# A mixed attention and state-space model on one core: input tables of the recurrence layer made in the projection in front, recurrence on pairs of blocks, and each feed-forward layer's modulation vectors summed within it

## The chip, the cores and the metric

The kernel runs on one core of a Trainium2 chip. The metric is the device time of one execution in microseconds (us), taken as the median of several runs. The core has four compute engines with a queue each: TensorE (PE, matrix products; PEld is its weight load), VectorE (DVE), ScalarE (ACT) and GpSimd (POOL). SyncE (SP) issues transfers. Engines run in parallel and order themselves by semaphores.

## The reference, cut to what matters

Ten layers work on 512 tokens of width 1024 in float32: feed-forward (f), latent attention with a short convolution (m), a mixer with two attentions (e) and one with a retention and a linear state-space recurrence (o). Their order is f0 m1 f2 f3 m4 f5 e6 f7 o8 f9. Every layer normalises, scales by (1 + scale) and shifts; its result is added with a gate. Shift, scale and gate (each 1024 long) are products of an activated vector `c` with a matrix, so 28 vectors of 1024 x 1024 matrix work beside the layers.

```python
for l in range(DEPTH):
    mod = jnp.split(c_act @ w_ada[l] + b_ada[l], N_MOD, axis=-1)
    h = modulate(rms_norm(x, ffn1_norm[l]), mod[0], mod[1])
    x = x + 0.5 * (1 + mod[2])[:, None, :] * swiglu(h, ffn1_w_gu[l], ffn1_w_down[l])
    ...
# the state-space part of the recurrence layer: 32 groups of 16 channels, 64 complex states each
a_bar = jnp.exp(lam * step)
b_bar = ((a_bar - 1.0) / lam)[..., None] * b
bu = jnp.einsum('gnp,blgp->blgn', b_bar, u)
states: s[t] = a_bar * s[t-1] + bu[t]
y = jnp.einsum('gpn,blgn->blgp', c, states).real + d_skip * u
```

Beside it in the same layer: retention over four heads (scores times a decay table, times values), a gate, a gated linear unit on y, and the output projection.

## The kernel before, in words

All weights stream through two slots `raw` of 128 x 1024 (a unit, 512 KB). Float32 products are made as three products of rounded parts: ScalarE rounds a unit to `w_hi` (`split_hi`), VectorE subtracts to `w_lo` (`split_lo`), TensorE multiplies (`mm3`: 24 matmuls of 128x512 a unit, about 5.45 us at the full clock). A unit's w_hi may be written once the unit two before is used, so each of the three engines has about one unit of time for its part, and an engine that is late with unit n stops TensorE at unit n.

A feed-forward layer has a hidden loop (`pe_ffn`, `dve_ffn`, 22 hidden tiles, two units each) and an output projection (`pe_out`, `act_out`, `dve_out`: 8 tiles of three units, after each tile x gets its addition, the next layer's rounded input and the sum of squares are begun). The next layer takes this input before the norm is known (`pair_pe`) and the rest behind it.

The modulation vectors are summed on GpSimd (`mod_sums`, lines 636 to 680): for each of a layer's jobs (vector j of set s) eight tiles of 128x1024 are loaded through two slots `mod_w`, multiplied by a column (L671, the first one L667 into the accumulator) and added to `mod_acc` (L674, L677), which has three slots, by j. A tile is fetched one ahead within a vector, and the first of the next only when the last vector is summed. GpSimd starts when the layer's last low part of the normalised input is made. VectorE folds each finished vector in the hidden loop, behind fixed hidden tiles (`FOLD_AT`: 6, 9, 12, 15, 18, 21; L593 transposes, L594 sums 32 columns); TensorE spreads the folded ones (`mod_spread`) and VectorE turns them to coefficients (`mod_coef`) behind the hidden loop. Before, layer 0 has seven jobs, layers 2, 5 and 7 six, layer 3 three, layer 9 none; the last job of the long lists is folded in the output projection.

In the recurrence layer (`pe_odd`, `act_odd`, `dve_odd`, and `pool_odd` for its transfers) 16 projection units of the input stream run with the state-space work between them. 512 tokens are 64 blocks of eight (`HOP`). Tables: `s_pw` powers of a_bar, `s_g` their products with the input factor (both made in the output projection of f7 by `state_powers`), `s_m` (input weights: `weights`, L2057 twice and L2495, plus a copy of the last power to `s_fb`), turned by TensorE (L2210) and read to `s_w`; `s_ca` (output weights, `readout`, 12 operations). `inputs` (L2226) multiplies the tables with the layer's input, which went through DRAM for a new layout (L2149, L2154), to one state input per block. `scan` (L2520 to L2528) carries the 128 x 32 states over the blocks: two products, two sums per step, each waiting for the one before. `taps` (L2239) makes the within-block kernel, that also goes through DRAM (L2163, L2167); `outputs` (L2259, L2263) needs it and the states. `scores`, `decay` (L2551), `retain` are the retention; `rotate` makes its rotary products from `swap_halves`. All orders on the four queues are written out by hand; `dve_odd` has the scan in pieces between the splits of later units.

## Time and profile before

| | us |
|---|---|
| median of 3 runs | 3488.41 |
| lowest and highest | 3487.97, 3494.15 |
| the profiled execution | 3492.11 |
| its span in the trace | 3489.3 |
| busy: TensorE, VectorE, ScalarE, GpSimd | 3284.6, 1866.2, 1181.4, 984.8 |

In the trace hidden loops of f0, f2, f5 and f7 run from about 66, 720, 1734 and 2438 us, the output projection of f7 from about 2680, the recurrence layer from 2805 to 3061, f9 from there to the end. Times in brackets in a row are the idle time of the engine just before it and who ended it. A matmul's own duration is longer than its share, since matmuls overlap.

### The profile page before, as it was taken

To read this page: it belongs to the slowest core of one execution; us is meant where nothing else is said; L and a number is where in the kernel's file an instruction comes from. 1 tells how busy PE (TensorE), PEld (TensorE's weight loads), DVE (VectorE), ACT (ScalarE), POOL (GpSimd) and SP (SyncE) were. 2 spreads that over 40 slices of the span, in tenths; PEclk is the share of its full clock that TensorE was granted. 3 is DMA by queue.
4 is the path that set the end of the run, shared out by engine and by line. 5 is a ranking of instruction groups with operands and counts; after the bars stand their busy time and mean duration, and the time that the engine had idled before them with its cause. 6 is when DMAs were issued, how large, how long until landed. Compare 5 with 4: busy or idle time off the path is not lost.

```text
span 3489.3 us, 40287 instructions
## 1 busy us (share of the span) xinstructions
PE 3284.6 (94%) x14477; PEld 2616.8 (75%) x14477; DVE 1866.2 (53%) x2573; ACT 1181.4 (34%) x1778; POOL 984.8 (28%) x675
## 2 busy tenths in 40 slices
PE   6999999999999999999999998989999988899998
PEld 4887875678787888775788776757777876778887
DVE  5565455656445533555655443256677486264443
ACT  3222243532223222335422223354333231243332
POOL 2888000068803700000088600000886000000000
PEclk7999999999999999999999998989999997799999
DMA  6665342156634633331266533202665333123332
GB/s 207 204 196 178 94 133 62 37 173 198 193 97 140 192 96 93 83 87 31 85 198 199 158 95 103 79 1 72 188 199 164 94 115 67 50 84 95 97 91 90
DMA packets 576560, 420.29 MB, mean 120 GB/s; under 512 B 28716, under 2 KB 535963, under 8 KB 575303
## 3 DMA queue, kind: packets, MB, share of 16 engines
q1 hardware_dynamic: 537330, 286.09, 27.9%
q0 software_dynamic: 33952, 122.70, 11.9%
q10 hardware_dynamic: 5172, 10.17, 0.9%
q8 instruction: 58, 0.95, 0.1%
q14 instruction: 48, 0.39, 0.0%
HBM read 413.10 MB, written 8.68 MB: 121 GB/s over the span
## 4 chain that ended last, share of the span: by engine, by line
PE 62%; POOL 15%; DVE 12%; issue 4%; ACT 3%; DMA 3%; ACTq 0%; SPq 0%; DVEq 0%; POOLq 0%
PE bank L324 18%; PE bank L326 17%; PE bank L325 17%; POOL mod_acc L674 8%; POOL mod_w L671 4%; PE bank L1306 2%; POOL mod_w L643 2%; DVE tmp L449 2%; DMA mod_w<-in_w_ada 2%; PE bank L1337 2%; DVE w_lo L305 1%; DVE h_lo L459 1%; POOL mod_acc L677 1%; PE bank L1327 1%; PE bank L430 1%
## 5 line engine op out<-in xcount | busy, mean ns | idle before, releaser
L324 PE MATMUL bank<-h_hi,w_hi 128*128 128x512 f32 x2656 | 1054.1, 397 | 62.3 <-DVE w_lo L305 25.5
L325 PE MATMUL bank<-h_lo,w_hi 128*128 128x512 f32 x2656 | 1043.4, 393 | 0.0
L326 PE MATMUL bank<-h_hi,w_lo 128*128 128x512 f32 x2656 | 1042.9, 393 | 0.0
L305 DVE TENSOR_TENSOR w_lo<-raw,w_hi 128x1024 fp32r<-128x1024 f32 x438 | 650.6, 1486 | 539.1 <-ACT w_hi L288 536.9
L288 ACT ACTIVATE w_hi<-raw 128x1024 fp32r<-128x1024 f32 x438 | 462.1, 1055 | 657.0 <-PE bank L326 654.6
L324 PEld LDWEIGHTS bank<-h_hi,w_hi 128*128 128x128 f32 x2656 | 503.0, 189 | 196.5 <-issue 45.7
L326 PEld LDWEIGHTS bank<-h_hi,w_lo 128*128 128x128 f32 x2656 | 502.8, 189 | 107.9
L325 PEld LDWEIGHTS bank<-h_lo,w_hi 128*128 128x128 f32 x2656 | 503.1, 189 | 102.5
L674 POOL TENSOR_TENSOR mod_acc<-mod_acc,mod_w 128x1024 f32<-128x1024 f32 x168 | 456.3, 2716 | 14.0
L324 PE MATMUL bank<-hid_hi,w_hi 128*128 128x512 f32 x1056 | 413.9, 392 | 7.1 <-DVE w_lo L305 7.1
L326 PE MATMUL bank<-hid_hi,w_lo 128*128 128x512 f32 x1056 | 412.1, 390 | 0.0
L325 PE MATMUL bank<-hid_lo,w_hi 128*128 128x512 f32 x1056 | 412.1, 390 | 0.0
L643 POOL DMA_DIRECT2D mod_w<-in_mod_w x96 | 56.6, 589 | 1000.0 <-DVE h_lo L459 975.7
L671 POOL TENSOR_SCALAR mod_w<-mod_w,cact 128x1024 f32<-128x1024 f32 x196 | 264.2, 1348 | 13.0 <-DMA mod_w<-in_w_ada 2.2
L296 DVE TENSOR_TENSOR w_lo<-raw,w_hi 128x1024 fp32r<-128x1024 f32 x92 | 112.5, 1224 | 265.9 <-ACT w_hi L279 265.4
L643 POOL DMA_DIRECT2D mod_w<-in_w_ada x128 | 75.3, 588 | 595.7 <-DVE h_lo L459 560.7
L324 PEld LDWEIGHTS bank<-hid_hi,w_hi 128*128 128x128 f32 x1056 | 198.9, 188 | 50.1 <-DVE w_lo L305 8.7
L326 PEld LDWEIGHTS bank<-hid_hi,w_lo 128*128 128x128 f32 x1056 | 198.9, 188 | 41.8
L325 PEld LDWEIGHTS bank<-hid_lo,w_hi 128*128 128x128 f32 x1056 | 199.0, 188 | 41.0
L1171 DVE TENSOR_TENSOR hid_lo<-hid,hid_hi 128x512 fp32r<-128x512 f32 (+1 forms) x127 | 169.3, 1333 | 36.6 <-ACT hid_hi L1090 36.6
L1166 DVE TENSOR_TENSOR hid<-act_t,bank 128x512 f32<-128x512 f32 x127 | 86.8, 683 | 151.5 <-PE bank L326 151.5
L1086 ACT ACTIVATE act_t<-bank 128x512 f32<-128x512 f32 x85 | 50.8, 598 | 321.4 <-PE bank L326 321.3
(339 smaller groups left out, 3262.4 us busy)
## 6 DMA issues: line engine op xcount, KB each, us to landing
raw<-in_ffn_w_gu SPq DMA_DIRECT2D x176, 512.0 KB, 4.0
mod_w<-in_w_ada POOLq DMA_DIRECT2D x128, 512.0 KB, 4.0
mod_w<-in_mod_w POOLq DMA_DIRECT2D x96, 512.0 KB, 4.2
raw<-in_ffn_w_in SPq DMA_DIRECT2D x88, 512.0 KB, 3.7
raw<-in_ffn_w_down SPq DMA_DIRECT2D x64, 512.0 KB, 3.5
raw<-in_w_in SPq DMA_DIRECT2D x34, 512.0 KB, 3.7
raw<-in_ffn_w_out SPq DMA_DIRECT2D x32, 512.0 KB, 3.5
raw<-in_ffn_w_down SPq DMA_DIRECT2D x32, 384.0 KB, 3.1
```

Source lines behind the costliest of these rows:

```text
L288: loop(nc.scalar.activation(w_hi[:, u % 2, :], raw[:, u % 2, :], ACT.Copy), "split_hi", times)
L296: done(nc.vector.tensor_tensor(w_lo[:, u % 2, :], raw[:, u % 2, :], w_hi[:, u % 2, :].bitcast(F32), ALU.subtract), "split_lo")
L305: loop(nc.vector.tensor_tensor(w_lo[:, u % 2, :], raw[:, u % 2, :], w_hi[:, u % 2, :].bitcast(F32), ALU.subtract), "split_lo", times)
L324: nc.tensor.matmul(dst, a_hi, b_hi, start=start, stop=False)
L325: nc.tensor.matmul(dst, a_hi, b_lo, start=False, stop=False)
L326: return nc.tensor.matmul(dst, a_lo, b_hi, start=False, stop=stop)
L449: done(nc.vector.scalar_tensor_tensor(tmp[:, m % 3, :], src(m), gain(m), inv, ALU.mult, ALU.mult), "norm_scaled", (key, m))
L643: pool.dma_start(mod_w[:, slot, :], src).then_inc(sg.sem(f"mod_loaded{slot}"), 16)
L671: done(pool.tensor_scalar(w, w, c, 1.0, ALU.mult, ALU.mult), "mod_step")
L674: done(pool.tensor_tensor(acc, acc, w, ALU.add), "mod_step")
L1166: loop(nc.vector.tensor_tensor(hid[:, jj, :], act_t[:, jj, :], psum[up][:, :], ALU.mult), "pair_evac", times)
L1171: loop(nc.vector.tensor_tensor(tile(hid_lo, i * 2 + jj), hid[:, jj, :], tile(hid_hi, i * 2 + jj).bitcast(F32), ALU.subtract), "hid_lo", times)
```

## The change

Modulation: every feed-forward layer now makes its own gate, and shift and scale (and for a mixer the gate too) of the sets that follow. Layers 0, 2, 5 and 7 have six jobs, layer 3 three, layer 9 one; all are folded in the hidden loop. The accumulator has two slots in turn, the tile buffer three, and tiles are fetched two ahead, across vectors. Recurrence layer: the four input tables are made in the output projection of f7, behind the splits 1, 2, 4, 5 of its second pair of tiles, into four slots of their own; the copies to s_fb are dropped (taps reads the tables); `combine` first makes each block's input that of two blocks, then the scan goes on pairs of blocks with the squared factor, in 31 steps; the orders on TensorE, ScalarE and VectorE are written anew.

```diff
-        mod_acc = place("mod_acc", [P, 3 * D])
-        mod_w = place("mod_w", [P, 2, D])
+        mod_acc = place("mod_acc", [P, 2 * D])
+        mod_w = place("mod_w", [P, 3, D])
...
         def mod_jobs(key):
-            if key[0] != "f" or key == final:
+            if key[0] != "f":
                 return []
             n = ORDER.index(key[1])
-            if n == 0:
-                return [(0, 2)] + [(t, j) for t in (ORDER[1], ORDER[2]) for j in range(3)]
-            ahead = {("f", 2): (1, 2), ("f", 3): (2,), ("f", 5): (1, 2), ("f", 7): (1, 2)}[key]
-            return [(ORDER[n + k], j) for k in ahead for j in range(3)]
+            jobs = [(ORDER[n], 2)]
+            for t in (n + 1, n + 2):
+                kind = [k for k, s in PHASES if k != "b" and t < len(ORDER) and s == ORDER[t]]
+                if kind == ["f"]:
+                    jobs += [(ORDER[t], 0), (ORDER[t], 1)]
+                elif kind and not (t == n + 1 and n and ("f", ORDER[n - 1]) in PHASES):
+                    jobs += [(ORDER[t], j) for j in range(3)]
+            return jobs
...
+        def mod_sums(pool, key):
+            for n, (s, j) in enumerate(jobs):
+                if n == 0:
+                    wait(pool, "norm_lo", (key, KT - 1))
+                    fetch(0, 0)
+                    fetch(0, 1)
+                if len(turn.former) >= 2:
+                    wait(pool, "mod_folded", turn.former[-2])
+                turn.former.append((s, j))
+                for t in range(KT):
+                    if t + 2 < KT:
+                        fetch(n, t + 2)
+                    elif n + 1 < len(jobs):
+                        fetch(n + 1, t + 2 - KT)
...
             def body(i, times):
-                if isinstance(i, int) and i == 2 and len(jobs) > 3:
-                    mod_fold(dve, key, len(jobs) - 1)
-                if isinstance(i, int) and i == 3 and len(jobs) > 3:
-                    mod_coef(dve, jobs[-1][0], [0, 1, 2], 7)
+                if isinstance(i, int) and i == 3 and len(sets) > 2:
+                    mod_coef(dve, sets[2], set_parts(key, sets[2]), 7)
...
+                        if ahead and isinstance(i, int) and i == 1 and k in (1, 2, 4, 5):
+                            state_weights(dve, nxt, (1, 2, 4, 5).index(k))
...
-            folding = FOLD_AT[:len(jobs) - (len(jobs) > 3)]
+            folding = FOLD_AT[:len(mod_jobs(key))]
...
+                cmul((den, t), power(HOP), power(HOP), s_t[:, :, 0])
+        def state_weights(dve, nxt, x):
+            part, js = x // 2, slice(8 * (x % 2), 8 * (x % 2) + 8)
+            if x == 0:
+                wait(dve, "b_loaded", nxt)
+            m = [s_m[:, i, :].rearrange("p (j k c) -> p j k c", j=8, k=HOP) for i in (x, 4)]
+            for i in range(2):
+                tt(m[i], spread(s_g[:, (i + part) % 2, js, :], 3, 16), spread(s_b[:, i, js, :], 2, HOP))
+            done(nc.vector.tensor_tensor(m[0], m[0], m[1], ...), "weights_ready", (nxt, x))
...   (pe_odd)
             readout()
-            weights(0)
+            for x in range(4):
+                weights(x)
             unit(4)
-            weights(1)
             unit(5)
+            inputs()
+            wait(pe, "out_ready", key)
             swap_halves(0)
-            weights(2)
+            swap_halves(1)
             unit(6)
-            wait(pe, "out_ready", key)
-            swap_halves(1)
-            weights(3)
-            inputs()
+            swap_halves(2)
             unit(7)
-            swap_halves(2)
             swap_halves(3)
+            wait(pe, "rotated", (key, 1))
             unit(8)
...   (dve_odd)
+            def combine():
+                n = BLOCKS - 2
+                former, now = s_s[:, :, :, 1:BLOCKS - 1], s_s[:, :, :, 2:BLOCKS]
+                vstep(nc.vector.tensor_tensor(s_q[:, 0, :, :, :], former, spread(s_a[:, 0, 0, :, :], 3, n), ALU.mult))
+                vstep(nc.vector.tensor_tensor(s_q[:, 1, :, :, :], swapped(former, n), spread(s_a[:, 0, 1, :, :], 3, n),
+                                              ALU.mult))
+                vstep(nc.vector.tensor_tensor(now, now, s_q[:, 0, :, :, :], ALU.add))
+                vstep(nc.vector.tensor_tensor(now, now, s_q[:, 1, :, :, :], ALU.add))
...
-            weights(0)
             split_lo(dve)
-            weights(1)
-            split_lo(dve)
-            weights(2)
-            split_lo(dve)
-            rotate(0)
-            weights(3)
-            split_lo(dve)
-            rotate(1)
             readout(0)
             split_lo(dve)
             readout(1)
+            split_lo(dve)
+            split_lo(dve)
             wait(dve, "input_read", (key, 3))
-            scan(2, 6)
+            combine()
+            split_lo(dve)
+            rotate(0)
+            rotate(1)
             split_lo(dve)
             rotate(2)
-            scan(6, 8)
             rotate(3)
-            scan(8, 11)
+            scan(0, 3)
             split_lo(dve)
-            scan(11, 16)
+            scan(3, 7)
             split_lo(dve)
-            scan(16, 21)
+            scan(7, 12)
             split_lo(dve)
-            scan(21, 37)
+            scan(12, 20)
             split_lo(dve)
-            scan(37, 42)
+            scan(20, 25)
             split_lo(dve)
-            scan(42, 47)
-            split_lo(dve)
+            scan(25, STEPS)
             wait(dve, "decay_loaded", key)
             wait(dve, "taps_stored", key)
             decay(0)
-            scan(47, 50)
             decay(1)
-            scan(50, BLOCKS)
+            split_lo(dve)
             gate_head(0)
```

ScalarE reads the eight table banks in one piece behind unit 3 and the state inputs behind unit 5. `scan(first, last)` now counts steps, each over blocks i and i + 1 with i = 3 + 2 * step.

## Rows read from the trace of the kernel before

**Rows 1.** The page: busy time, share of the span and instructions of each engine.
```profile
PE 3284.6 (94%) x14477; PEld 2616.8 (75%) x14477; DVE 1866.2 (53%) x2573; ACT 1181.4 (34%) x1778; POOL 984.8 (28%) x675
```
**Rows 2.** Who waited for whom, whole span: total us, times, longest.
```profile
DVE tmp L593 <- POOL mod_acc L677: 17.7, 3, 7.1
```
**Rows 3.** Timeline of TensorE, recurrence layer: start, us, instructions, [idle before, releaser].
```profile
2876.38 0.80 PE L356 MATMUL bank<-w_hi,h_hi 128*128 128x512 f32 x1 [5.02 <-DVE w_lo L296]
...
2918.20 2.42 PE L2273 MATMUL bank<-o_qk 64*128 64x512 f32 x8
2926.74 4.63 PE L2273 MATMUL bank<-o_qk 64*128 64x512 f32 x8 [6.11 <-DVE o_w L2551]
...
2943.49 3.65 PE L2259 MATMUL bank<-s_u,s_taps 128*128 128x64 f32 x16 [5.25 <-DVE s_s L2528]
...
2964.26 4.77 PE L2263 MATMUL bank<-s_s,s_ca 64*128 64x64 f32 x32
...
2983.19 7.09 PE L2263 MATMUL bank<-s_s,s_ca 64*128 64x64 f32 x32
```
**Rows 4.** Windows: stretch, us, busy time of each engine, granted clock, DMA.
```profile
2860.00:2880.00 20.00, 14.98 (x55) 11.05 (x54) 19.24 (x39) 2.60 (x3) 0.00 (x0) 0.87 0.17 53
...
2920.00:2940.00 20.00, 12.13 (x28) 6.97 (x27) 12.65 (x60) 2.25 (x3) 0.00 (x0) 0.66 0.28 75
```
**Rows 5.** Timeline of VectorE, projection of f7 and recurrence layer.
```profile
2703.38 0.23 DVE L2057 TENSOR_TENSOR s_pw<-s_pw 128x64 f32<-128x64 f32 x1
...
2847.33 2.48 DVE L2057 TENSOR_TENSOR s_m<-s_g,s_b 128x1024 f32<-128x1024 f32 x2
...
2872.16 0.20 DVE L2520 TENSOR_TENSOR s_p<-s_s,s_a 128x32 f32<-128x32 f32 x1
...
2872.89 0.20 DVE L2520 TENSOR_TENSOR s_p<-s_s,s_a 128x32 f32<-128x32 f32 x1
```
**Rows 6.** Timeline of GpSimd, then the issues of all transfers (KB, median us to landing).
```profile
2837.81 5.00 POOL L2154 DMA_DIRECT2D s_u<-bias_skewed_rows  x8 [5.95 <-DMA bias_skewed_rows<-o_u]
...
s_u<-bias_skewed_rows POOLq DMA_DIRECT2D x8, 128.0 KB, 4.2
```
**Rows 7.** Who waited for whom: GpSimd's first product of a vector.
```profile
POOL mod_acc L667 <- DMA mod_w<-in_w_ada: 45.4, 16, 3.2
```
**Rows 8.** Timelines in layer 2: VectorE, GpSimd's last addition, TensorE behind the fifth fold.
```profile
923.70 1.25 DVE L593 STREAM_TRANSPOSE tmp<-mod_acc 128x1024 f32<-128x1024 f32 x1 [7.12 <-POOL mod_acc L677]
...
951.78 0.69 DVE L1171 TENSOR_TENSOR hid_lo<-hid,hid_hi 128x512 fp32r<-128x512 f32 x1
...
962.56 3.25 POOL L677 TENSOR_TENSOR mod_acc<-mod_acc,mod_w 128x1024 f32<-128x1024 f32 x1
...
927.47 0.49 PE L324 MATMUL bank<-h_hi,w_hi 128*128 128x512 f32 x1 [2.97 <-DVE w_lo L305]
```
**Rows 9.** Layer 0, behind the hidden loop: timeline of TensorE and one window.
```profile
315.72 0.79 PE L324 MATMUL bank<-hid_hi,w_hi 128*128 128x512 f32 x1 [4.46 <-DVE w_lo L305]
...
346.07 0.51 PE L324 MATMUL bank<-hid_hi,w_hi 128*128 128x512 f32 x1 [2.37 <-DVE w_lo L305]
...
300.00:320.00 20.00, 15.47 (x62) 12.35 (x59) 12.22 (x16) 4.98 (x6) 16.00 (x11) 0.87 0.53 163
```
**Rows 10.** Layers 7 and 9: VectorE at their starts, TensorE behind a fold.
```profile
2435.90 1.62 DVE L459 SCALAR_TENSOR_TENSOR h_lo<-tmp,coef,h_hi 128x512 fp32r<-128x512 f32 x2
...
2446.01 3.36 DVE L305 TENSOR_TENSOR w_lo<-raw,w_hi 128x1024 fp32r<-128x1024 f32 x1
...
2458.87 1.64 DVE L305 TENSOR_TENSOR w_lo<-raw,w_hi 128x1024 fp32r<-128x1024 f32 x1 [0.96 <-ACT w_hi L288]
...
2588.41 0.49 PE L324 MATMUL bank<-h_hi,w_hi 128*128 128x512 f32 x1 [1.97 <-DVE w_lo L305]
...
3123.17 1.62 DVE L459 SCALAR_TENSOR_TENSOR h_lo<-tmp,coef,h_hi 128x512 fp32r<-128x512 f32 x2
...
3140.39 1.23 DVE L305 TENSOR_TENSOR w_lo<-raw,w_hi 128x1024 fp32r<-128x1024 f32 x1 [2.28 <-ACT w_hi L288]
```

More of the change, by code:

```diff
@@ L2530, in scan @@
-                    if i < BLOCKS - 1:
+                    ins = nc.vector.tensor_tensor(now, now, p2, ALU.add)
+                    final_step = step == STEPS - 1
+                    done(ins, "scanned" if final_step else "scan_step", key if final_step else None)
+                    if not final_step:
                         dve.wait_ge(sg.sem("scan_step"), sg.count["scan_step"])
```

172 lines of the change are left out of this document (75 added, 97 removed).

## The prediction

> **What bounds the kernel now.** I read the page first. TensorE is busy for 94% of the span and no other engine reaches 60% [rows 1], so only three things can shorten the time: fewer idle gaps of TensorE, more of it at the higher clock, or fewer matrix columns. The change leaves the columns alone. TensorE has 205 us without work. Second view, who waited for whom: most of TensorE's waits are for VectorE, above all for w_lo, the low parts of the weights, and VectorE in turn stood 17.7 us, three times, before a fold of a modulation vector that GpSimd had not finished [rows 2]. Third, TensorE's timeline, read only for rows with a bracket: the recurrence layer (about 2805 to 3061) has the largest cluster, 5.02 us before a w_lo, 6.11 us before a decay product, 5.25 us before the end of the recurrence [rows 3]. The clock says more than the gaps: the granted clock was 0.87 of 2.4 GHz between 2860 and 2880 and 0.66 between 2920 and 2940, that is for two thirds of that stretch at the lower level of 1.2 GHz [rows 4]. The same eight score matmuls took 2.42 us without and 4.63 us behind the 6.11 us gap [rows 3].
>
> **Part 1, the recurrence layer.** VectorE's queue is the cause of these gaps. Before, it holds four input tables of three 1024-element operations each (1.24 us apiece) with a short copy, 4 x 3.9 = 15.7 us; then 62 steps of four dependent 32-element operations, one step every 0.73 to 0.75 us, 46 us [rows 5]. After, the tables are gone from here; the steps are 31 on 64 elements; four products and sums over 1984 elements come first. A 64-element operation took 0.23 us against 0.20 for 32 [rows 5], so I take 0.85 us a step: 26 us. The four large ones by the rate of the 1024-element row, 2.2 us each: 9 us. VectorE loses 15.7 + 46 - 35 = 27 us. (The Trainium skill, Vector Engine (DVE) Microarchitecture Reference, section 5.2, has pairs of words that start on an odd word at 1.30 ns a column and a hop at every element at up to 1.98. The pairs here start at odd blocks. By that a step on pairs costs only 4 x 20 ns over one on single blocks, 0.83 us, and a large operation 2.7 us rather than 2.2; the sum would move by 1 us. No row here shows odd pairs.)
>
> What TensorE gets of it, walked unit by unit with the rows' durations. Up to the third projection unit behind the values: the 5.02 us wait, one of 1.06 behind it and the slow restart (0.13 of 20 us [rows 4] and, by my estimate, 0.8 behind it, 3.4 us) go, 9.5 us in all. New small waits come in their place: all eight table transposes now stand in one piece and are read by ScalarE one by one (1 us); unit 5's w_lo is queued behind the first readout (0.7 us); the half swap directly behind unit 6 waits for ScalarE's evacuation (0.8 us); unit 8 may not start until the second rotation, behind which VectorE now has the four large operations (0.5 us). Net -6.5 us. Then the scores: the decay product is no longer queued behind a w_lo that waits for a late load, so the gap of 6.11 becomes the 1.7 us that the product itself takes, -4.3; the second scores at full speed, -2.2; the recurrence ends some 10 us before it is needed, so the 5.25 us wait goes. Sum -18.3. The retention matmuls behind (about 7 us) have run at the lower clock; no row decides whether gaps of 1.7 us let it fall, so I count most of half their time, -3. The output products of the state stay at the lower level: a block of them took 7.09 us with full-speed work and no gap two blocks in front of it [rows 3]. Part 1: -21, with ends at -8 (every saved gap is half refilled) and -35 (the higher clock holds through the output products too).
>
> Of the steps that move: the matmuls that apply the tables now come one unit earlier, at about 2848. Their input is loaded by GpSimd's eight transfers, issued 2837.8 to 2842.8 with a median of 4.2 us to landing [rows 6]; they land at about 2848. This is hidden by nothing any more: it costs 0 to 1 us, and each us that they are late stalls TensorE and, through the wait for the products, VectorE with all splits behind it.
>
> **Part 2, the tables in the projection in front.** Twelve operations of 1.24 us stand between the splits of the second pair of output tiles (near 2710). A table is 3.7 us. One unit of TensorE is 5.45 us, ScalarE and VectorE need 2.5 of it, so 2.9 are free: a table overruns this by 0.8, and where the tile's addition comes next (2.9 us) its split comes 1 us late. Twice: +2 us (0 to 6). Ten more operations of 0.2 us for the squared factor are hidden. The two loads of b are landed some 9 us before their first use.
>
> **Part 3, the modulation vectors.** GpSimd waits for the first tile of each vector, 45.4 us in 16 times for one of the two sources [rows 7], 2.9 us each. Fetching two ahead removes it for all but the first vector of a layer: five times 3.0, so the sixth ends 15 us earlier. In layer 2 the fifth fold waited 7.12 us, TensorE 2.97 behind it [rows 8]. GpSimd then ends the fifth 12 us earlier: the wait is gone. But the sixth fold moves from the output projection into the hidden loop at tile 21. Without the 2.97 VectorE is there at 952.4 - 3.0 = 949.4 [rows 8]; GpSimd, that ended at 965.8, ends at 950.8. VectorE waits 1.5 us, folds 2.5, makes four coefficient parts in 1.7 and splits; TensorE needs that split at about 957.3 and gets it then. I allow 0.6 us. Layers 2 and 5: -2.3 each, -4.6.
> Layer 0: the first gap (4.46 us) stands behind the last fold, for which VectorE waited 17.7 - 2 x 7.12 = 3.5 us [rows 2, 9]; it shrinks to 0.6. The stretch at 0.87 [rows 9] gives 2.6 back and what lies behind it, again by estimate, 0.8. The 2.37 us gap [rows 9] falls into the seventh vector's time, when GpSimd slows w_lo; the seventh vector has left this layer. -3.9 - 3.4 - 2.4 = -9.7.
> Layer 7 (with the convolution) folds five vectors in its hidden loop and stalls each time, 1.97 us in the row shown [rows 10]; a sixth is added: +1.7.
> Layer 9 gets a vector of its own, so GpSimd works in its first 40 us, which it did not. The twin is layer 7: there w_lo took 3.36 us beside GpSimd's additions, and the split that follows the first converted pair came at 2458.87, 21.4 us after the end of the last h_lo; in layer 9 at 3140.39, 15.6 us after [rows 10]. That is +5.8 if all of it is GpSimd; layer 9 entered at the lower clock, so I take +5, and +1.6 for its fold. +6.6. (The Trainium skill, SBUF - State Buffer, section "SBUF: two separate sides", has this as an exclusive lock between GpSimd and a VectorE operation with two SBUF inputs, held for the whole instruction. It speaks against putting any of GpSimd's work beside a start that is tight. By that rule a w_lo could wait for a whole addition at each step; the trace has it at 3.36 against 1.24 us.)
> Part 3: -4.6 - 9.7 + 1.7 + 6.6 = -6.0.
>
> **Sum.** -21 + 2 - 6.0 = -25 us on the profiled execution's 3492.1 (span 3489.3 and 2.8 around it): 3467.1. The median of the runs is 3.7 below this execution, so 3463.4.
>
> **The rivals.** (a) The clock stays up: the recurrence layer no longer stands idle for more than 3 us before the output products, and these and the two projection units between them run at 2.4 GHz. For it: the second block of output products took 4.77 us right after a full-speed unit [rows 3]. Against it: the later ones took 7.09 with no gap in front [rows 3]. Price: three blocks at 3.5 to 4 us, two units at 2.5: -10 to -17 more, 3446 to 3453. (b) New waits take the place of the old: input_loaded lands 2 to 5 us late, the values' read, the gate of the second rotation, and each gap over 2.5 us pays 1.4 to 3.4 us of slow clock. Part 1 shrinks to -8, the total to -8 to -14: 3474 to 3480. (c) The state path from taps to projection outputs (two round trips through DRAM) sets the layer's end whatever VectorE does; part 1 is near 0, and layer 7 and 9's losses eat the rest: within 7 us, about 3485. Against it: TensorE waited for VectorE and not for a load in the rows of group 3. (d) Slower: GpSimd does not get faster, because its two loads in flight share the DMA engines with the weights and land later, or because its operations are held up by VectorE as long as they save. Then the sixth fold at tile 21 in layers 2 and 5 finds its vector 965.8 - 949.4 = 16.4 us late, all inside a loop in which TensorE has 4 us of cover (7.12 us of waiting cost 2.97): 12.4 + 3.4 of slow clock, twice, +32; against -25 + 4.6 for the rest this ends at +11, 3500. It decides as soon as a vector takes over 38.8 us on average (40.9 now, 38.4 by my sum); at 39.5 it costs 8 us. (e) The change does not do what it says: the tables or coefficients are made later than used and a semaphore wait shows it; the order of the queues leaves no such wait that I can find, and it would look like (c).
>
> **Chances.** Forecast 0.55; (a) 0.17; (b) 0.14; (c) with (e) 0.08; (d) 0.06. A measurement of this kernel can tell about 0.2%, 7 us, from no change. Faster: forecast, (a), (b) = 0.86; within: 0.08; slower: 0.06. The forecast's own bounds are 3453 to 3475; the range takes in all of (a) but its best end and (b): 3446 to 3480, which leaves out (c), (d) and a sliver, under 2 in 10.
>
> **What would show it.** In the recurrence layer: no TensorE gap over 2.5 us before the output products except the one at the values' read, which the change does not touch; first output products near 2925 + the shift from before; scanned no releaser of TensorE. Vectors of GpSimd 37 to 38 us apart, with no wait at their first product but in the first of a layer; VectorE's wait before folds at most 2 us. In layer 9 a gap of some 4 us at its start. Wrong if: the step on pairs takes over 1.1 us; if the eight input loads release TensorE; if the clock before 3000 is near 1.0, which is (a); if w_lo waits in layer 7's output projection exceed 3 us each.

## The result and the profile after

The kernel after takes 3458.61 us (median of four runs, 3449.83 to 3465.99) beside 3491.28 of before, a ratio of 0.9905 (95% interval 0.9878 to 0.9932). Run again on another chip it was 3454.08 beside 3496.27, 0.9880 (0.9864 to 0.9897). The forecast was 3463.4 with a range of 3446 to 3480 and 0.86 on faster: both hold. As a change the forecast was -25 us, and the medians moved by -32.7 and -42.2, each beside before on its own chip: a ratio of 0.9928 was forecast, which lies within the first interval and outside the second. The profiled execution is the fastest of its four runs (3449.83, span 3448.0), 41.3 us of span less than before's.

Where these 41.3 us lie is read by layer, from the first product with `sq` (the sums of squares that open a norm) to the next one; layer 0 is counted from 66 us into the span, where its hidden loop starts. Times in us, each from one profile:

| layer | before | after | after, again | forecast of the change | change measured |
|---|---|---|---|---|---|
| 0 | 370.3 | 359.0 | 358.9 | -9.7 | -11.3, -11.4 |
| 2 | 375.2 | 368.8 | 370.7 | -2.3 | -6.4, -4.5 |
| 5 | 372.5 | 366.1 | 367.2 | -2.3 | -6.4, -5.3 |
| 7 | 386.7 | 395.1 | 393.4 | +3.7 | +8.4, +6.7 |
| 8 (recurrence) | 300.3 | 278.2 | 277.9 | -21 | -22.1, -22.4 |
| 9 and the end | 383.4 | 386.5 | 384.2 | +6.6 | +3.1, +0.8 |
| 1, 3, 4, 6 | 1234.8 | 1228.3 | 1229.2 | 0 | -6.5, -5.6 |

The layers with a term add up to -34.7 in the first profile and -36.1 in the second, where the sum was -25. The last row is 7.6 and 6.2 us of layer 4 with a little of the others the other way; no line of the change runs in layer 4, and it took 262 to 270 us in kernels that have the same code in it, so I count it as chance. Layer 3, whose three vectors are now requested ahead too, stayed at 368.4 and 369.0 for 368.5.

The page of after, busy time of each engine (answers to [rows 1]: VectorE lost 54.7 us and 114 instructions, TensorE 15.8 us with the same products to make; the page counts 40 matmuls more, as some records are missing in a trace), and who waited for whom (answers to [rows 7]; in the list of VectorE's waits no wait for a fold is left, [rows 2] had 17.7 us):

```profile
PE 3268.8 (95%) x14517; PEld 2605.8 (76%) x14517; DVE 1811.5 (53%) x2459; ACT 1179.8 (34%) x1778; POOL 977.5 (28%) x675
...
POOL mod_acc L686 <- DMA mod_w<-in_w_ada: 9.1, 4, 2.5
```

TensorE's timeline in the recurrence layer (answers to [rows 3]), with two 20 us windows (stretch, length, TensorE busy, granted clock as a share of 2.4 GHz, DMA share, GB/s):

```profile
2827.25 3.95 PE L2254 MATMUL bank<-s_u,s_w 128*64 128x64 f32 x128 [1.27 <-DMA s_u<-bias_skewed_rows]
...
2878.31 0.79 PE L325 MATMUL bank<-h_hi,w_hi 128*128 128x512 f32 x1 [2.69 <-ACT o_v L2416]
...
2890.98 2.42 PE L2302 MATMUL bank<-o_qk 64*128 64x512 f32 x8
2895.27 4.63 PE L2302 MATMUL bank<-o_qk 64*128 64x512 f32 x8 [1.88 <-DVE o_w L2579]
2899.83 5.69 PE L2312 MATMUL bank<-o_w,o_v 128*128 128x512 f32 x16
2905.36 1.90 PE L2288 MATMUL bank<-s_u,s_taps 128*128 128x64 f32 x16
2907.19 5.53 PE L2292 MATMUL bank<-s_s,s_ca 64*128 64x64 f32 x32
...
2938.72 7.09 PE L2292 MATMUL bank<-s_s,s_ca 64*128 64x64 f32 x32
```
```profile
2903.00:2923.00 20.00, 20.00 (x113) 0.83 0.10 27
2923.00:2943.00 20.00, 20.00 (x105) 0.57 0.19 53
```

The gaps of 5.02 and 5.25 us are gone, and the one of 6.11 is 1.88. The loads of the input now release TensorE, 1.27 us late (in the second profile of after no such gap is left). The second scores still took 4.63 us, the lower level of 1.2 GHz. The first output products start 122.0 us into the layer, 137.9 before: -15.9; the other -6.2 come behind them.

VectorE in the same layer (answers to [rows 5]): a large operation of the pairs, one step on 64 elements and the start of the next, the last steps, the decay product.

```profile
2831.87 2.22 DVE L2533 TENSOR_TENSOR s_q<-s_s,s_a 128x1984 f32<-128x1984 f32 x1 [1.24 <-ACT s_s L2446]
...
2853.04 0.23 DVE L2546 TENSOR_TENSOR s_p<-s_s,s_a 128x64 f32<-128x64 f32 x1
2853.18 0.22 DVE L2548 TENSOR_TENSOR s_p<-s_s,s_a 128x64 f32<-128x64 f32 x1
2853.32 0.28 DVE L2552 TENSOR_TENSOR s_s<-s_s,s_p 128x64 f32<-128x64 f32 x1
2853.63 0.28 DVE L2555 TENSOR_TENSOR s_s<-s_s,s_p 128x64 f32<-128x64 f32 x1
2853.95 0.27 DVE L2546 TENSOR_TENSOR s_p<-s_s,s_a 128x64 f32<-128x64 f32 x1
...
2893.27 0.21 DVE L2555 TENSOR_TENSOR s_s<-s_s,s_p 128x32 f32<-128x32 f32 x1
2893.53 1.69 DVE L2579 TENSOR_TENSOR o_w<-bank,tmp 128x512 f32<-128x512 f32 x4
```

### The profile page after: what moved, and what is told of

Read it like the earlier page. It is cut to its first block, busy times and chain, and to the rows that moved or that the text cites. A ratio compares the mean times of both kernels' runs of the same rounds, so it can differ in the third digit from the quotient of the medians.

```text
span 3448.0 us, 40289 instructions
## 1 busy us (share of the span) xinstructions
PE 3268.8 (95%) x14517; PEld 2605.8 (76%) x14517; DVE 1811.5 (53%) x2459; ACT 1179.8 (34%) x1778; POOL 977.5 (28%) x675
## 4 chain that ended last, share of the span: by engine, by line
PE 82%; DVE 11%; ACT 4%; issue 2%; DMA 1%; ACTq 0%; POOL 0%; SPq 0%; DVEq 0%; POOLq 0%
PE bank L325 24%; PE bank L326 24%; PE bank L327 24%; PE bank L1326 2%; PE bank L1357 2%; DVE tmp L450 2%; DVE w_lo L306 1%; DVE h_lo L460 1%; PE bank L1347 1%; PE bank L431 1%; DVE folded L510 1%; DVE w_lo L297 1%; PE bank L2292 1%; PE bank L409 1%; ACT w_hi L280 1%
## 5 line engine op out<-in xcount | busy, mean ns | idle before, releaser
L289 ACT ACTIVATE w_hi<-raw 128x1024 fp32r<-128x1024 f32 x438 | 462.1, 1055 | 654.7 <-PE bank L327 654.7
L693 POOL TENSOR_TENSOR mod_acc<-mod_acc,mod_w 128x1024 f32<-128x1024 f32 x168 | 432.3, 2573 | 14.0
L690 POOL TENSOR_SCALAR mod_w<-mod_w,cact 128x1024 f32<-128x1024 f32 x196 | 272.6, 1391 | 9.5
L327 PEld LDWEIGHTS bank<-hid_hi,w_lo 128*128 128x128 f32 x1056 | 198.4, 188 | 41.3
L280 ACT ACTIVATE w_hi<-raw 128x1024 fp32r<-128x1024 f32 x92 | 96.9, 1054 | 147.0 <-PE bank L327 80.6
## 6 DMA issues: line engine op xcount, KB each, us to landing
raw<-in_ffn_w_down SPq DMA_DIRECT2D x32, 384.0 KB, 3.0
```

The costliest lines, as they stand in the source:

```text
L280: done(nc.scalar.activation(w_hi[:, u % 2, :], raw[:, u % 2, :], ACT.Copy), "split_hi")
L289: loop(nc.scalar.activation(w_hi[:, u % 2, :], raw[:, u % 2, :], ACT.Copy), "split_hi", times)
L327: return nc.tensor.matmul(dst, a_lo, b_hi, start=False, stop=stop)
L690: done(pool.tensor_scalar(w, w, c, 1.0, ALU.mult, ALU.mult), "mod_step")
L693: done(pool.tensor_tensor(acc, acc, w, ALU.add), "mod_step")
```

## The experiments

The layer lengths of all runs, in us, each from one profiled execution ("as after" where within 2 us of either profile of it). Each run's comparison with the kernel before was made on its own chip.

| kernel | 0 | 2 | 5 | 7 | 8 | 9, end | ratio to before (95%) |
|---|---|---|---|---|---|---|---|
| vectors alone | 358.2 | 370.8 | 366.0 | 391.5 | 298.9 | 386.8 | 0.9927 (0.9908 to 0.9946) |
| recurrence alone | 374.3 | 375.2 | 372.4 | 390.7 | 275.9 | 383.4 | 0.9945 (0.9928 to 0.9962) |
| tables back | as after | as after | as after | 391.0 | 285.7 | 384.1 | 0.9882 (0.9865 to 0.9899) |
| single steps | as after | as after | as after | 393.7 | 293.2 | 384.2 | 0.9896 (0.9876 to 0.9915) |
| order of before | as after | as after | as after | 395.1 | 288.5 | 386.5 | 0.9917 (0.9896 to 0.9939) |
| sixth fold later | as after | as after | as after | 395.2 | 278.1 | 386.4 | 0.9894 (0.9877 to 0.9910) |
| no request ahead | 360.0 | 382.9 | 379.3 | 390.0 | 277.8 | 386.5 | 0.9954 (0.9936 to 0.9972) |
| early scores | as after | as after | as after | 395.1 | 268.5 | 389.2 | 0.9877 (0.9860 to 0.9893) |
| mixed blocks | as after | as after | as after | 395.2 | 271.5 | 384.3 | 0.9850 (0.9829 to 0.9870) |
| no ninth vector | as after | as after | as after | 395.4 | 278.0 | 383.4 | 0.9866 (0.9846 to 0.9886) |
| after, again | 358.9 | 370.7 | 367.2 | 393.4 | 277.9 | 384.2 | 0.9880 (0.9864 to 0.9897) |
| best | 358.1 | 369.9 | 368.0 | 387.6 | 271.9 | 384.0 | 0.9820 (0.9798 to 0.9841) |

The ratios of kernels that should differ by 3 us do not order themselves (tables back, 0.9882, stands below after's first 0.9905, on another chip): the attention layers move by up to 8 us from execution to execution, and the median of before itself is 3491 to 3501 us from chip to chip. The other layers repeat within 2.5 us where their code is the same, but for layer 0 of the second kernel (374.3 for 370.3) and layer 9, told below, so the verdicts go by the layer that an edit touches. A difference of 2 us in one layer is no finding by itself. I had expected the second profile of after within 1 us of the first in layers 2, 5, 7, 8 and 9, and only layer 8 was.

**The two halves.** The first kernel has the diff's vector hunks with the old recurrence layer, the second the other hunks with the old vectors.

```
# first kernel: no tables in layer 7
+            repeat(dve, 4, body, first=ahead, last=True, alone=())
...
# second kernel: the last fold ahead of the tables
+                if isinstance(i, int) and i == (1 if ahead else 2) and len(jobs) > 3:
+                    mod_fold(dve, key, len(jobs) - 1)
```

> The changed modulation vectors alone (part 3 of the change), with the recurrence layer and layer 7's output projection of the kernel before. Theory: the stages that differ between the two profiles belong to the change and add up: layer 0 -11, layers 2 and 5 -6.5 each, layer 7 +8.4 less some 2.5 for the tables in its output projection, so +6, layer 9 +2: -16 us, ratio 0.9954. My prediction's own sum for this part was -6 us, 0.998: it holds if the -6.5 in layers 2 and 5 (I had -2.3) were the luck of one profile. In the profile: GpSimd's wait at the first product of a vector gone for all but the first vector of a layer, as in the kernel after.

> Parts 1 and 2 alone: the recurrence on pairs, the tables in layer 7's output projection, the new order in the recurrence layer; the modulation vectors as before, but that layer 7's sixth fold stands one pair of output tiles earlier, ahead of the tables (their places overlap). Theory: -22 in layer 8 and +2 to +3 in layer 7: -19 to -20 us, 0.9944. If this and the first run do not add up to the change's -33 us, the parts depend on each other. Rival: if GpSimd has to end its sixth vector for the fold that now comes earlier (it ended at about 2682, the fold stands near 2700), VectorE waits there and layer 7 costs up to 8 us: -14.

The halves add up layer by layer, to within 4 us: layer 7 pays 4.8 for the vectors and 4.0 for the tables (8.4 and 6.7 together), layer 8 is -24.4 with the recurrence part and -1.4 without (-22.1 together), layers 2 and 5 change with the vectors alone, and layer 0 is 4.0 longer in the second kernel, which changes nothing in it. The second kernel's ratio came as expected (0.9945 for 0.9944); the first's, 0.9927, is 9 us below its 0.9954, and its layers do not show these 9 us. The vectors alone are worth -14.8 over their five layers, near the -16 of the theory and not the -6 of the prediction: -12.1, -4.4, -6.5, +4.8 and +3.4, so the gain in layers 2 and 5 is no luck of one profile, but for 2 of the 6.4 us of layer 2. The feared wait at the earlier fold did not show.

**The tables, back in the recurrence layer.**

```
             vstep(nc.vector.memset(s_s[:, :, :, 0:1], 0.0))
+            for x in range(4):
+                state_weights(dve, key, x)
             split_lo(dve)
```

> The kernel after, but the four input tables (12 operations of 1.24 us, 14.9 us) are made in the recurrence layer, all four ahead of the first split behind the norm. Theory (VectorE's queue is what TensorE waits for up to the values): TensorE waits for nearly all of it, 12 to 15 us ahead of unit 4, and pays the slow clock behind so long a gap: +14 to +19 us against the kernel after, of which 2.5 come back in layer 7: ratio to before 0.994 to 0.996. Rival (the state path with its two round trips through DRAM sets the end of the layer, and VectorE has 45 us without work behind the recurrence): the late start is mostly absorbed, +3 to +7 only, ratio 0.991 to 0.993.

Layer 8 is 7.5 us longer and layer 7 4.1 shorter: moving 14.9 us of VectorE out was worth 3.4 us (5.4 by the second profile of after, whose layer 7 took 393.4). Neither theory has it; it is near the upper end of the rival's, whose ratio (0.991 to 0.993 for 0.9882) did not come either. At the values the layer stands at 102.3 us for 95.0, so the loss is made up front (TensorE waits 2.69 us for a table and 2.71 for a w_lo, and no longer for the input loads) and not given back later, as the rival had it. The other half of the 14.9 us must lie in idle time that VectorE had there; that is a reading, no run measures it.

**The pairs.** Same stretches between the same splits, 62 steps instead of four large operations and 31.

```
-                for step in range(first, last):
-                    i = 3 + 2 * step
+                for step in range(2 * first, 2 * last):
+                    i = 2 + step
...
-            combine()
```

> The kernel after, but the recurrence goes over single blocks again: 62 steps of four 32-element operations in place of four operations over 1984 elements and 31 steps on 64 elements, cut into the same stretches between the same splits. VectorE gets 46 us of steps for 36 us. Theory: the work fits either way, the recurrence ended about 12 us before the first output product, so at most the stretches between splits overrun: +2 us (0 to 5), ratio to before 0.991. Rival (the pairs are what made the gain): each split behind a stretch comes 1 to 3 us late, TensorE waits for w_lo about 8 times and then for the recurrence's end: +10 us or more, ratio 0.9935 or more.

The rival holds in its size: +15.0 in the layer. Its ratio, 0.9935, did not come: 0.9896 lies 14 us lower and by itself does not tell this kernel from after, so the finding rests on the layer's length in one profile and on the rows below. Its mechanism did not come either: of the eight late splits one shows (1.49 us, in the unit behind the restart at the values), and the end of the recurrence releases nothing on TensorE. TensorE's timeline of that kernel, then VectorE's:

```profile
2906.23 2.07 PE L2302 MATMUL bank<-o_qk 64*128 64x512 f32 x2 [10.74 <-DVE o_w L2579]
```
```profile
2904.38 0.21 DVE L2555 TENSOR_TENSOR s_s<-s_s,s_p 128x32 f32<-128x32 f32 x1
2904.51 1.67 DVE L2579 TENSOR_TENSOR o_w<-bank,tmp 128x512 f32<-128x512 f32 x4
```

The steps end 120.7 us into the layer for 110.2 and the first decay product with them: 10.74 us of gap for 1.88, +8.9, and slower retention and output products behind the gap. The slack I had seen, from the end of the recurrence to the first output product, was not there to be spent: the decay products stand behind the last step in VectorE's queue, and in after they start with no idle time at 2893.53, 0.1 us after the scores they read were done.

**The order.** Tables ahead and pairs kept, the front of the layer in the old order on three engines.

```
-            for x in range(4):
-                weights(x)
-            unit(4)
-            unit(5)
-            inputs()
...
+            weights(3)
+            inputs()
+            unit(7)
```

> The kernel after, with the tables still made ahead and the recurrence still on pairs, but TensorE, ScalarE and VectorE go through the front of the recurrence layer in the order of before (tables transposed one by one between the units, input products behind unit 6, rotations ahead of the readout tables). Stage lengths so far: this layer 278.2 us in after, 293.2 with single steps, 285.7 with the tables back, 300.3 before; pairs -15.0 and tables -7.5 make the whole -22.1, so nothing is left for the order. Theory: the order alone is worth 0 to 3 us, layer 278 to 281. Rival (the large combining operations need the input early, and behind unit 6 they stand just ahead of a split that TensorE waits for): +6 to +10 us, layer 284 to 288, with a w_lo wait of 4 to 6 us at unit 8.

+10.3, again the rival, at its upper end and with a wait of 11.50 us where it had 4 to 6. TensorE, then VectorE, which reads the input only when it has made both readout tables, and then has four large operations ahead of the split:

```profile
2866.23 0.80 PE L357 MATMUL bank<-w_hi,h_hi 128*128 128x512 f32 x1 [11.50 <-DVE w_lo L297]
```
```profile
2846.55 1.22 DVE L297 TENSOR_TENSOR w_lo<-raw,w_hi 128x1024 fp32r<-128x1024 f32 x1
...
2855.92 2.22 DVE L2537 TENSOR_TENSOR s_q<-s_s,s_a 128x1984 f32<-128x1984 f32 x1
...
2864.95 1.23 DVE L297 TENSOR_TENSOR w_lo<-raw,w_hi 128x1024 fp32r<-128x1024 f32 x1
```

So -15.0 (pairs), -7.5 (tables) and -10.3 (order) are 32.8 us where the layer gained 22.1: each of the three needs the others, and an undo of one counts what the others lose by it.

**The vectors.** The sixth fold in the output projection, then no request for the next vector's tiles before the sum of the last.

```
-            folding = FOLD_AT[:len(mod_jobs(key))]
+            folding = FOLD_AT[:min(len(mod_jobs(key)), 5)]
```
```
-                    elif n + 1 < len(jobs):
-                        fetch(n + 1, t + 2 - KT)
```

> The kernel after, but the sixth fold of layers 0, 2, 5 and 7 stands in the output projection (first pair of tiles in layer 7, second in the others) rather than at tile 21 of the hidden loop. Its coefficients are wanted only at the last pair. Layer 7 is 391.5 us with the changed vectors alone and 386.7 before, +4.8. Theory: the sixth fold in the hidden loop is 2.5 us of VectorE where nothing covers it; layer 7 becomes 2 to 3 us shorter (392 to 393) and layers 2 and 5 gain 0.5 to 1 each: -4 us in all. Rival (the +4.8 comes from GpSimd's denser operations slowing w_lo through the loop, not from the fold): layer 7 stays within 1 us of 395.1.

> The kernel after, but a vector's first two tiles are requested only when the vector before it is summed, as in the kernel before: GpSimd waits some 3 us per vector again, while the sixth fold stays at tile 21. This is what my rival (d) priced: layers 2 and 5 with the sixth vector 13 to 16 us late, 12.4 us of it uncovered and 3.4 us of slow clock. Theory (d's price): layers 2 and 5 +12 to +16 each (381 to 385 against 368.8 and 366.1), layer 0 +8 to +14, layer 7 +10 or more, +40 to +50 us in all, ratio to before 1.002 to 1.005. Rival (the late fold is partly covered, since only one split stands behind it and two units of TensorE are already fed): half of that, ratio about 0.997.

The fold's place is worth nothing (layer 7 395.2 for 395.1). Without requests ahead, layers 2 and 5 lose 14.1 and 13.2 us beside after, inside the 12 to 16 expected, but the whole kernel is at 0.9954 where 1.002 to 1.005 was expected and the rival had 0.997. In layer 2, TensorE and VectorE of that kernel:

```profile
958.06 0.79 PE L325 MATMUL bank<-hid_hi,w_hi 128*128 128x512 f32 x1 [7.97 <-DVE w_lo L306]
```
```profile
952.30 1.25 DVE L606 STREAM_TRANSPOSE tmp<-mod_acc 128x1024 f32<-128x1024 f32 x1 [10.78 <-POOL mod_acc L694]
```

All of VectorE's waits for GpSimd (28.6 us, four times) lie in these two layers. Layer 0 lost 1 us, no fold being late there, and layer 7 gained 5.1 (3.4 beside the second profile of after). Its gaps are as long with requests ahead as without (0.81, 2.28, 1.68, 1.77, 1.66 against 0.73, 1.19, 1.72, 1.70, 2.02, 1.66 behind its start), but the clock is not. Windows of after, then of the kernel without requests ahead:

```profile
2548.22:2568.22 20.00, 17.72 (x72) 0.91 0.67 207
...
2588.22:2608.22 20.00, 18.32 (x82) 1.00 0.68 210
...
2628.22:2648.22 20.00, 20.00 (x83) 0.91 0.35 105
```
```profile
2575.92:2595.92 20.00, 18.28 (x81) 1.00 0.54 168
...
2635.92:2655.92 20.00, 17.98 (x80) 1.00 0.68 218
```

Twice in after the clock falls, at a price of some 1.8 us each (9% of 20), behind the gap of 2.28 and behind that of 1.77; other gaps of that size cost nothing. That is 3.6 of the 4.8 us that the vectors cost this layer, and the same two windows stand in the run with the vectors alone. The second profile of after has two such falls as well, behind gaps of 2.30 and 1.90. The rest of the 5.1 is the start, where TensorE waited 3.98 us for 5.33; that is no effect of the edit, since the second profile of after has 3.88 there. Beside that profile layer 7 gained 3.4 us, about what the two falls cost. Which gap the fall of the clock takes hold of, no run tells.

**Layer 9.** Its vector left out:

```
-            if key[0] != "f":
+            if key[0] != "f" or key == final:
```

> The kernel after, but layer 9's own gate vector is left out (its eight tiles, their sum, fold and coefficients; the layer uses old coefficients). From the start of layer 9 to the end: 383.4 us before, 386.5 after, but 384.1 to 389.2 in the other kernels that have the vector. My prediction had +6.6 for the vector (5 at the start, 1.6 for the fold). Theory: without it 383.4 again, so the vector costs some 3 us, and the first w_lo wait of the layer is about 1 us for 2.2. Rival (my price was right, and something else in after gave part of it back): below 381.

> The kernel after itself, once more, on the chip of the two others: as the base for them, and to see which stage lengths repeat. Expected: layers 2, 5, 7, 8 and 9 within 1 us of the first profile (368.8, 366.1, 395.1, 278.2, 386.5 with the end), the attention layers 1 and 4 within 8; ratio to before 0.990 to 0.991.

The layer then works with old coefficients. 383.4 without the vector, 384.2 in after on the same chip and 386.5 in its first profile: it costs 1 to 3 us. The first w_lo wait of the layer, in after, in its second profile, without the vector, and in the kernel of the early scores:

```profile
3090.42 0.49 PE L325 MATMUL bank<-h_hi,w_hi 128*128 128x512 f32 x1 [2.17 <-DVE w_lo L306]
```
```profile
3091.04 0.49 PE L325 MATMUL bank<-h_hi,w_hi 128*128 128x512 f32 x1 [0.90 <-DVE w_lo L306]
```
```profile
3103.66 0.49 PE L325 MATMUL bank<-h_hi,w_hi 128*128 128x512 f32 x1 [0.92 <-DVE w_lo L306]
```
```profile
3084.65 0.79 PE L325 MATMUL bank<-h_hi,w_hi 128*128 128x512 f32 x1 [5.38 <-DVE w_lo L306]
```

One and the same kernel waits 2.17 us in one execution and 0.90 in another. Of the eight other profiles in which the vector begins at the layer's start, three have 0.88 to 1.21, four 2.12 to 2.53 and one 5.38; the kernels without the vector have 0.86 to 0.92. So the price of GpSimd's start beside the layer's start is not a number but a range, from nothing to 4.5 us, and its +5 was the upper end. The 0.92 of this run alone does not show that the vector made the 2.17.

**Scores early, blocks mixed.** A change of order behind the values, then a second one among the output products.

```
             unit(11)
+            wait(pe, "values_read", (key, 1))
+            wait(pe, "taps_read", key)
+            scores(0)
             unit(12)
+            scores(1)
             unit(13)
```
```
             outputs(1)
...
+            scores(2)
+            unit(15)
+            outputs(2)
+            scores(3)
+            retain(2)
+            outputs(3)
```

> The kernel after with another order behind the values: TensorE makes the first scores ahead of unit 12 and the second between units 12 and 13 (and the third ahead of unit 15), and VectorE makes the decay products there, ahead of the last stretches of the recurrence. Theory (the clock is lost by gaps: 2.69 us at the values, 1.88 at the decay product): both gaps shrink by 1 to 2 us, the second scores run at 2.4 GHz (2.42 us for 4.63) and the retention products behind them, so the layer is 6 to 9 us shorter, 269 to 272. Rival (the clock falls because of the small products themselves, and the recurrence now ends later): only the gaps go, -2 to -4, and the first output product waits for the recurrence: layer 275 to 278.

> The kernel of the early scores, and in addition the last two blocks of output products no longer stand together: TensorE goes block 1, third scores, unit 15, block 2, fourth scores, third retention product, block 3, fourth retention product. In the early-scores run TensorE had no gap from 2880 on, and yet its granted clock was 0.83 and 0.50 in the stretches with the output products: blocks took 7.1, 5.7, 9.8 and 10.8 us (1.9 + 3.8 at 2.4 GHz). Theory (the clock follows what TensorE does, and a block made of small products lowers it for what comes behind it, while products of 512 columns between them bring it back): blocks 2 and 3 at 5.7 to 7.1 us each, layer 268.5 less 6 to 9: 260 to 262. Rival (the state path: the second half's round trip through DRAM starts 0 to 3 us later and now ends last): the gain in TensorE becomes a wait before the gated products, layer 265 to 269.

The early scores gave -9.6 (268.5), a little over their theory: the first output product comes 118.4 us into the layer for 122.0, and from there to the sums of squares (`sq`) of its end it takes 58.3 us for 63.7. But the clock fell in the output products all the same, with no gap over 0.6 us behind the values. Of that kernel:

```profile
2919.03 3.78 PE L2292 MATMUL bank<-s_s,s_ca 64*128 64x64 f32 x32
2922.74 2.69 PE L2288 MATMUL bank<-s_u,s_taps 128*128 128x64 f32 x16
2925.36 7.09 PE L2292 MATMUL bank<-s_s,s_ca 64*128 64x64 f32 x32
```
```profile
2924.00:2944.00 20.00, 20.00 (x90) 0.50 0.18 52
```

With products of 512 columns between the blocks they took 6.8, 7.2, 5.6 and 7.5 us in place of 7.0, 5.6, 9.7 and 10.7: 5.9 us less, as the clock theory had it. But most of that went to the 512-column products between them. The stretch from the first output product to the sums of squares holds the same products in both kernels and no gap, here with the early scores alone, then mixed:

```profile
2902.87:2961.18 58.31, 58.31 (x275) 0.71 0.21 63
```
```profile
2910.62:2966.72 56.10, 56.10 (x275) 0.73 0.11 33
```

So the order was worth 2.2 us of TensorE, not 5.9, and it raised the granted clock of the stretch from 0.71 to 0.73. The layer still became 3.0 us longer than with the early scores alone. The last block now ended later, and VectorE of that kernel waited for the second half's round trip through DRAM, and TensorE behind it (3.28 us in the kernel without mixing):

```profile
2973.43 1.41 DVE L2566 SCALAR_TENSOR_TENSOR o_u<-o_u,cols,o_state 128x512 f32<-128x512 f32 x2 [19.32 <-DMA o_state<-bias_skewed_rows]
```
```profile
2978.70 5.89 PE L431 MATMUL bank<-ident,stat 128*128 128x128 f32 x32 [7.60 <-DVE stat L1854]
```

That is the mixed kernel's rival, 2.5 us worse than its own range.

**The best version.** Early scores; layer 7 without requests ahead and with one table in each half of two pairs of output tiles; layer 9's vector behind the third hidden tile.

```
+            cross = key != ("f", 7)
...
+                    if key == final:
+                        pool.wait_ge(sg.sem("hid_lo"), at("hid_lo", (key, "base")) + 3)
...
-                        if ahead and isinstance(i, int) and i == 1 and k in (1, 2, 4, 5):
+                        if ahead and isinstance(i, int) and i in (1, 2) and k in (0, 3):
...
-            folding = FOLD_AT[:len(mod_jobs(key))]
+            folding = [12] if key == final else FOLD_AT[:len(mod_jobs(key))]
```

> The early scores (layer 8 at 268.5 us for 278.2) and three edits around the vectors: layer 7 requests a vector's first tiles only when the one before is summed (390.0 us against 395.1 in the run without requests ahead), its four tables stand one in each half of the second and third pair of output tiles (theory: 0.8 us late each, with two units to catch up, so most of the 4.1 us of the tables go), and layer 9's vector starts behind the third hidden tile and is folded at the twelfth (theory: the w_lo wait at the layer's start, 5.38 us with the early scores, 2.17 in after, goes down to the 0.92 of the run without the vector, and only the fold stays). Expected by this: layer 7 at 387 to 388, layer 8 at 268 to 270, layer 9 with the end at 384 to 385; 3430 to 3437 us, ratio to before 0.981 to 0.984. Rival (these prices do not add up, since the clock at each entry depends on where the gaps fall): as the early scores alone, 0.9877, to 0.985.

3437.78 us beside 3499.90, 0.9820, just over the 3430 to 3437 expected and inside the ratios: the prices nearly hold together, layer 7 at 387.6 (its clock 1.00 in every 20 us window behind the start) and layer 9 at 384.0 as expected (its w_lo wait 0.88 us, which after itself had in its second profile, so that the later start of the vector is not shown to have made it), layer 8 at 271.9 for 268 to 270. The waits of 1.39 and 1.10 us that the tables had put in front of TensorE in layer 7's output projection are gone.

## Why the prediction was right, and where it was not

**Part 1, -21 against -22.1: right total, wrong places.** Up to the restart behind the values -5.1 (I had -6.5: the new small waits came to 4.3 us for 3.0, 1.27 of them the input loads), the decay gap -4.2 (-4.3), the second scores 0 (-2.2: a gap of 1.88 behind a restart left them at 4.63 us), retention 5.69 us for about 7, -1.3 (-3), the recurrence's end -5.25 (-5.25): -15.8, where the first output products stand 15.9 earlier. My terms gave -21.3 at that point. In the second profile they stand 14.5 earlier, retention takes 7.37 us and gains nothing, and 7.9 come behind it: the total repeats, the split does not. The other -6.2 of the first profile came behind it, where I had counted nothing: the first block took 7.4 us for 10.7, the unit and block behind it the rest. That is a piece of rival (a), which I had given 0.17 for -10 to -17. That it made up for what my terms had too much is luck. My reason was wrong too. I held the clock up or down by gaps; the run with early scores has no gap in this stretch and 0.50 of the clock, and the one with mixed blocks has its blocks faster and what stands between them slower, so the small output products themselves lower it. The Trainium skill, TensorE: Matmul & The Clock Gate, Part 1, ties the level to how busy TensorE was; here it was busy for 20.00 of 20 us at 0.50, so busy time by the profile alone does not say it.

**The recurrence's slack.** "Ends some 10 us before it is needed" was a wrong reading, which cost the forecast nothing since its 26 and 9 us of VectorE were right: 2.22 us for a large operation, 0.85 to 0.91 a step for 0.85. The slack was 0, at the decay product, as the run with single steps shows. The estimate of 2.7 us for a large operation, worked out from the figure of the Trainium skill, Vector Engine (DVE) Microarchitecture Reference, section 5.2, for pairs that start on an odd word, did not come: 2.22 us, with runs of 62 blocks that start at an odd one. The 64-element operations do alternate between 0.22 and 0.28 us.

**The input loads** did release TensorE, by 1.27 us for my 0 to 1 (not in the second profile). One of the four things named as "wrong if" thus happened, at a size that changes nothing.

**Part 2, +2 (0 to 6) against +3.6 to +4.1.** Mechanism right, size too small by half: two waits of 1.39 and 1.10 us and not two of 1, and the rest is not seen as a gap. What failed is the view that the tables had to leave: 14.9 us of VectorE in the recurrence layer cost 7.5 there.

**Part 3, -6.0 against -14.8** (vectors alone; -16.6 and -17.7 in the two profiles of after, less 4 for the tables). This is the step that failed. Layer 0: right (-11.3 for -9.7), both gaps gone to nothing. Layers 2 and 5: the fold's 2.97 went, but I had allowed 0.6 for the sixth fold, which costs nothing, and had not counted that a late w_lo elsewhere in the loop goes as well: before, four waits of 4.3 us in all in layer 2; after, none over 0.5 (in its second profile one of 0.71 at the start is back, and the layer is at -4.5 for -6.4). The 2 us between the profiles are the layer's start: TensorE's wait of 1.5 us for the normalised input ends 15.2 us into the layer in the first profile, 17.5 in the second and 17.7 before (in layer 5: 15.3, 16.8 and 17.7). As the same kernel has both, I count it as chance, and some 4 us in each of the two layers as the gain. The sixth sum is ready just in time. GpSimd's last addition in layer 2 of after, then VectorE:

```profile
934.71 3.29 POOL L696 TENSOR_TENSOR mod_acc<-mod_acc,mod_w 128x1024 f32<-128x1024 f32 x1
```
```profile
935.67 2.88 DVE L1190 TENSOR_TENSOR hid_lo<-hid,hid_hi 128x512 fp32r<-128x512 f32 x1
938.48 1.23 DVE L606 STREAM_TRANSPOSE tmp<-mod_acc 128x1024 f32<-128x1024 f32 x1
```

The sum ends at 938.00 and its fold starts 0.5 us later, with no wait in VectorE's list; but the operation in front of the fold took 2.88 us beside this addition, where [rows 8] had 0.69. So most of the lateness is hidden in that operation, and TensorE had cover for it.

Layer 7: +4.8 for +1.7; the fold was the wrong suspect, the clock's two dips are 3.6 of it. Layer 9: +0.8 to +3.1 for +6.6; "all of it is GpSimd" was the upper bound taken as the value.

**The rivals.** (c) did not come, nor did (b), whose new waits came to 4.3 us in all. Of (d), GpSimd at 40 us a vector and the sixth fold late, the run without requests ahead shows the mechanism and half the price. (d) had layers 2 and 5 at +16 each beside before; they are +7.7 and +6.8, since the sixth vector was 10.78 us late for 16.4, and 7.97 of them reached TensorE. The kernel is 0.9954 of before, 20 us faster, not slower: the rest, with the chance of layer 4 in it, gained 33. In after GpSimd took 37.7 us a vector in layer 2 (41.2 before), within the 37 to 38 forecast. The forecast lies 10 us above the layers' sum, and nearly all of that is part 3: -5 to -8 in layers 2 and 5, -3.5 to -5.8 in layer 9, -1.6 in layer 0, against +3.1 in layer 7. In the median the miss is 4.8 and 9.3 us, inside the range. As a change beside before on the same chip it is 7.7 and 17.2 us, since before itself came out slower than the 3488.4 that the forecast started from; that the second median lies so near the forecast is in part luck.

## What to carry to other kernels

Slack of a queue is read at the next instruction of that queue that somebody waits for, not at the consumer of the last result: look for the row that starts with no idle time. Price a move by both ends; what leaves a stage is worth what it blocked there, less what it blocks in the new place. And where short products stand together, look at the granted clock before the gaps, and judge another order by the whole stretch and not by the short products alone: here the blocks became 5.9 us shorter and the stretch 2.2.

## What the runs showed of the hardware

A run of 64-column products with 64 or 128 rows lowered TensorE's granted clock to 0.50 although TensorE had no idle time, and with 512-column products between the blocks the blocks were faster (5.6 us at best, 10.7 at worst) while those products were slower, so that the stretch took 56.10 us at 0.73 for 58.31 at 0.71. Gaps of 1.2 to 2.3 us in the same loop cost 0 or 1.8 us of slow clock, without a rule that the rows show. Nor does a longer gap settle it: behind the gap of 2.97 us in layer 2 of before, over which rival (b) would have had slow clock, the granted clock was 1.00, and behind that of 2.28 in layer 7 of after 0.79:

```profile
927.47:935.47 8.00, 8.00 (x35) 1.00 0.80 252
```
```profile
2556.68:2564.68 8.00, 8.00 (x28) 0.79 0.85 244
```

GpSimd's additions beside VectorE's w_lo took it to 3.4 us for 1.23, as [rows 10] had it, and at the start of layer 9 TensorE then waited anything from 0.9 to 5.4 us, 0.90 and 2.17 in two executions of the same kernel. That the rest is how the two fall together is a reading, which no run tests.
